# Inverse root mean squares of 128x640 blocks: logarithm and exponential on ScalarE in place of a square root there and a reciprocal on VectorE

## The reference, cut to what matters

```python
def rms_norm(x, g):
    y = xf * lax.rsqrt(jnp.mean(xf * xf, axis=-1, keepdims=True) + EPS)
    return (y * g.astype(jnp.float32)).astype(x.dtype)
...
    d = uf - jnp.mean(uf, axis=-1, keepdims=True)                       # group_layer_norm, 4 groups of 64
    y = (d * lax.rsqrt(jnp.mean(d * d, axis=-1, keepdims=True) + EPS)).reshape(bsz, t, ch)
...
    o_gla = rms_norm(o_f + jnp.flip(o_b, 1), p['gla_norm_g'][l]) * jax.nn.silu(heads(gg, GLA_DV))
    u = jax.nn.silu(group_layer_norm(u, p['conv_norm_g'][l], p['conv_norm_b'][l]))
    qa = rms_norm(heads(aq, HEAD_DIM), p['q_norm_g'][l])
    ka = rms_norm(heads(ak, HEAD_DIM), p['k_norm_g'][l])
```

## Time and profile before

| | before |
|---|---|
| median of three runs | 4559.03 us (4555.75 to 4562.23) |
| profiled execution, its own time | 4560.16 us |
| span of that execution | 4558.4 us |
| mean granted TensorE clock | 0.817 of 2.4 GHz |
| busy: PE, DVE, ACT, POOL | 2964.4, 2789.8, 954.6, 2699.0 us |
| DMA traffic | 1450.20 MB, mean 318 GB/s |

### The profile page before, as it was taken

How to read it: one execution, slowest core, us unless ns; L and a number is a source line. 1 busy time by engine, 2 the same in 40 slices (tenths; PEclk the granted TensorE clock), 3 DMA queues, 4 the chain that set the end, 5 groups by cost and what they waited for, 6 DMA issues and landing times.

```text
span 4558.4 us, 50026 instructions
## 1 busy us (share of the span) xinstructions
PE 2964.4 (65%) x17354; PEld 1289.0 (28%) x17354; DVE 2789.8 (61%) x6337; ACT 954.6 (21%) x2379; POOL 2699.0 (59%) x2760
## 2 busy tenths in 40 slices
PE   6997855566655565666578968455556665555555
PEld 4565521122211221222134655111212122212111
DVE  3515457667676677667535363676667766766673
ACT  2134012212221222122121331122122212211221
POOL 3700027777777777777748000577777777777775
PEclk9998678777788877877789968788878778888878
DMA  6532239999999999999931102799999999999998
GB/s 217 182 113 94 84 141 409 409 409 407 404 408 404 405 406 406 406 405 403 403 128 35 38 3 83 298 409 408 409 404 403 406 402 409 402 408 406 405 405 349
DMA packets 471181, 1450.20 MB, mean 318 GB/s; under 512 B 54165, under 2 KB 131345, under 8 KB 470801
## 3 DMA queue, kind: packets, MB, share of 16 engines
q0 software_dynamic: 368640, 1342.34, 74.4%
q1 hardware_dynamic: 102290, 104.66, 7.1%
HBM read 1443.62 MB, written 3.21 MB: 317 GB/s over the span
## 4 chain that ended last, share of the span: by engine, by line
PE 26%; DMA 23%; DVE 22%; POOL 15%; issue 11%; DVEq 2%; ACT 1%; SPq 0%; ACTq 0%; POOLq 0%
PE ps L551 25%; DMA arena<-in_peer_u,expert_rows 13%; DVE arena L1454 9%; DMA arena<-in_peer_v,expert_rows 9%; POOL arena L526 7%; POOL arena L534 7%; PE ps L686 1%; DVE arena L1402 1%; DVE arena L1371 1%; DVE top_indices L1401 1%; DVE arena L1433 1%; DVE arena L1436 1%; DVE chosen_pair L1438 1%; DVE top_values L1404 1%; DVE best_positions L1401 1%
## 5 line engine op out<-in xcount | busy, mean ns | idle before, releaser
L551 PE MATMUL ps<-arena 64*64 64x512 f32 (+5 forms) x14768 | 2740.3, 679 | 1430.7 <-issue 1175.7
L1454 DVE CUSTOM_DVE_ANT_0 arena<-arena,ps 128x1024 f32<-128x1024 f32 x1280 | 1526.7, 1219 | 891.3 <-DMA arena<-in_peer_u,expert_rows 887.9
L551 PEld LDWEIGHTS ps<-arena 64*64 64x64 f32 (+2 forms) x14768 | 1136.7, 179 | 3018.4 <-issue 2904.8
L526 POOL DMA_INDIRECT arena<-in_peer_u,expert_rows x1280 | 1217.9, 952 | 686.0 <-issue 306.7
L534 POOL DMA_INDIRECT arena<-in_peer_v,expert_rows x1280 | 1211.0, 946 | 412.2 <-issue 358.2
L1184 ACT ACTIVATE arena<-constants,expert_weight 128x64 f32<-128x64 f32 x1280 | 380.3, 339 | 1402.5 <-PE ps L551 1378.5
L513 POOL MEMSET arena<- 128x5632 f32 x2 | 9.6, 4792 | 372.8 <-ACTq L257 372.8
L1299 DVE TENSOR_REDUCE score_max<-ps 128x1 f32<-128x640 f32 (+1 forms) x80 | 57.4, 718 | 246.8 <-PE ps L551 246.8
L506 POOL TENSOR_SCALAR arena<-arena,vec_columns 128x512 f32<-128x512 f32 x120 | 150.4, 1264 | 10.2 <-issue 10.2
L515 POOL MEMSET arena<- 128x2048 f32 x2 | 3.6, 1806 | 226.7 <-DVEq L257 226.7
L1111 ACT ACTIVATE arena<-ps 128x256 f32<-128x256 f32 x80 | 30.7, 384 | 457.8 <-PE ps L551 444.2
(11 more groups left out here) (162 smaller groups left out, 1819.2 us busy)
## 6 DMA issues: line engine op xcount, KB each, us to landing
arena<-in_ada_w SPq DMA_DIRECT2D x40, 1024.0 KB
arena<-in_peer_u,expert_rows POOLq DMA_INDIRECT x1280
arena<-in_peer_v,expert_rows POOLq DMA_INDIRECT x1280
arena<-in_w_in SPq DMA_DIRECT2D x32, 512.0 KB, 4.1
arena<-in_ada_w SPq DMA_DIRECT2D x4, 2048.0 KB, 18.7
arena<-in_w_out SPq DMA_DIRECT2D x4, 2048.0 KB, 7.6
arena<-in_peer_wq SPq DMA_DIRECT2D x2, 4096.0 KB, 18.7
peer_modulation<-modulation_rows SPq DMA_DIRECT2D x4, 1536.0 KB, 11.5
```

The lines of the kernel that those rows point to most:

```text
L526: pool.indirect_dma_start(UR[:, k % RING, :], None, u_rows, bass.IndirectOffsetOnAxis(ap=rows[:, g % LIVE, k:k + 1], axis=0))\
L551: return pe.matmul(out, lhsT, rhs, start=start, stop=stop)
L1454: dve.tensor_tensor_reduce(out=UR[:, k % RING, :], in0=UR[:, k % RING, :], in1=pair(1), scale=1.0, scalar=0.0, op0=ALU.mult, op1=ALU.add, ...
```

## The change

The square root of mean plus epsilon becomes a logarithm, and a second activation raises e to minus a half of it, in place; that is the inverse root at once. DVE's reciprocal of the block goes. The small reciprocals (of 128x5 values, lines 1225 and 1482) and the square roots ahead of them stay.

```diff
                 def deviation(u):
                     act.wait_ge(S["var_ps"], NU * l + u + 1)
                     if u:
                         act.wait_ge(S["n_ready"], NU * l + u)
-                    act.activation(SD, pair(0)[:, 0:NTOK], ACT.Sqrt, bias=eps_c[:, 0:1]).then_inc(S["sd_ready"], 1)
+                    st.link(act.activation(SD, pair(0)[:, 0:NTOK], ACT.Ln, bias=eps_c[:, 0:1]))
+                    act.activation(SD, SD, ACT.Exp, scale=-0.5).then_inc(S["sd_ready"], 1)
...
                 for ct in range(2):
                     act.wait_ge(S["cx_var"], 2 * l + ct + 1)
-                    act.activation(CSQ[:, ct, :], zp(ct)[:, 0:NTOK], ACT.Sqrt, bias=eps_c[:, 0:1])\
-                        .then_inc(S["cx_sd"], 1)
+                    st.link(act.activation(CSQ[:, ct, :], zp(ct)[:, 0:NTOK], ACT.Ln, bias=eps_c[:, 0:1]))
+                    act.activation(CSQ[:, ct, :], CSQ[:, ct, :], ACT.Exp, scale=-0.5).then_inc(S["cx_sd"], 1)
...
                 for hp in range(2):
                     act.wait_ge(S["og_var"], 2 * l + hp + 1)
-                    act.activation(OSD[:, hp, :], pair(hp)[:, 0:NTOK], ACT.Sqrt, bias=eps_c[:, 0:1])\
-                        .then_inc(S["og_sd"], 1)
+                    st.link(act.activation(OSD[:, hp, :], pair(hp)[:, 0:NTOK], ACT.Ln, bias=eps_c[:, 0:1]))
+                    act.activation(OSD[:, hp, :], OSD[:, hp, :], ACT.Exp, scale=-0.5).then_inc(S["og_sd"], 1)
...
                     dve.wait_ge(S["sd_ready"], NU * l + u + 1)
-                    st.link(dve.reciprocal(SD, SD))
                     stt(src, src, vec[:, g:g + 1], SD, ALU.mult, ALU.mult).then_inc(S["n_ready"], 1)
...
                     dve.wait_ge(S["cx_sd"], 2 * l + ct + 1)
-                    st.link(dve.reciprocal(CSQ[:, ct, :], CSQ[:, ct, :]))
...
                     dve.wait_ge(S["og_sd"], 2 * l + hp + 1)
-                    st.link(dve.reciprocal(OSD[:, hp, :], OSD[:, hp, :]))
```

## The result

The changed kernel takes 4573.7 us (median of nine runs, 4568.63 to 4575.44), the kernel before 4559.72 (nine runs, 4555.75 to 4562.23): 14.0 us or 0.3% more, ratio 1.003 with a 95% interval of 1.002 to 1.004. The profiled execution took 4568.63 us, the shortest of the nine.

What follows compares the result with a forecast made beforehand. PE bounds the projections with ACT's root on its path, DVE bounds GLA, transfers the experts. Longer projections +25.0, GLA's first part -16.7, its end -7.6, clock +10.3 make +11.0: 4571.2 us, 4570 to compare; range 4551 to 4578.

Steps and rivals of the forecast that it cites:

- The bound and where the edits lie on it: Projections: PE bounds, with ACT's root on its path; GLA: DVE bounds; expert stages: transfers, untouched by the change.
- The reciprocals: 18 of 4.15 us each: nothing gained from the projections' ten; first part of GLA saves 8.36 us a layer, 16.7 in all.
- ACT's cover: First part of GLA: twelve exponentials start 3.1 us later yet end 4 us before DVE asks; failure costs at most 3.1 a layer.
- The tables: Logarithm and exponential evict each other, a 1.283 us load before nearly each, some 28 more; projection paths grow 25.0 us in all.
- The added load of the small root: Line 1140: about 1.3 us of load, taken as 0 because PE later waits for key copies; bounds 0 and 1.3 a layer.
- The end of GLA: Second reciprocal goes but ACT becomes late in DVE's place; 3.8 us saved a layer, 7.6 in both.
- The stalls: Projections: PE's eight waits for the inverse root become 5.04 us each, about 40 us in all.
- The clock: PE's clock falls behind the projections' eight stalls: 1.5 us each, bounds 0 and 1.7; net +10.3 us, between -1.7 and +11.9.
- the sum: Whole kernel: +25.0 - 16.7 - 7.6 + 10.3 = +11.0 us on the profiled 4560.16, giving 4571.2; time to compare 4570.
- The holding clock: Rival, chance 0.22: PE's clock stays at 2.4 GHz behind the projections' stalls; +0.7 or less, about 4559 us, no change.
- One table: Rival, chance 0.15: the build keeps one table with logarithm and exponential for projections and GLA; about 4538 us, faster.
- Dearer loads: Rival, chance 0.03: chained table loads cost twice the price for the 20 on the path; +26, about 4596 us.

Runs made afterwards that it cites:

- The filled stalls: Changed kernel with 16 unread PE products put into each of the four stalls of the second layer's projection; 4567.11 us, 1.0014 of the kernel before.
- the early release: Changed kernel, but PE's next mean of squares waits for the logarithm alone, not the exponential behind it; 4548.54 us, ratio 0.9976 to the kernel before.
- one table: Changed kernel with the table holding logarithm and exponential loaded three times a layer where ACT has time; 4533.88 us, ratio 0.9944 to the kernel before.
- one table in GLA alone: Kernel before with the change only in GLA, the table holding both functions loaded ahead of attention and behind line 1090; 4532.16 us, ratio 0.9942.

## Why the prediction was right, point by point

**The bound and where the edits lie on it.** PE in the projections and DVE in GLA, as read. The two kernels with half of the change each give +39.5 and -25.6 us.

**The reciprocals.** Nothing was to be gained from the ten in the projection, and nothing was: PE's stalls are all behind ACT. The first part of GLA was to save 8.36 us a layer; it saved 8.0 and 8.4. ACT's cover held: its twelve exponentials start 3.1 us later, as worked out (8.03 us behind the first running sum, 4.96 before), and no product of DVE waits for one.

**The tables.** 28 loads more (205 against 177), with the first logarithm of GLA finding its table loaded, as the argument from the earlier trace rows has it. The added load of the small root is hidden: PE still waits for the key copies there, 2.14 us as in the earlier trace rows. The Trainium skill, "ScalarE: Activation LUTs", section "Table sets: the hidden batching unit", says that one set holds logarithm and exponential; the trace with the set loaded by hand agrees, and in the changed kernel, where nobody asked for it, it wasn't used. The drain of about 1380 ns that the Trainium skill, "ScalarE: Activation LUTs", section "What ACT_TABLE_LOAD costs", adds to each load would have made the stalls 2 x 1.38 us longer. The trace disagrees: they are 5.04 or 5.03, without it.

**The end of GLA.** 3.8 us a layer were forecast and 3.9 measured.

**The stalls.** 5.04 us each and some 40 in all were forecast; eight of 5.04 or 5.03, 40.3 in all, were there.

**The clock is the term that was too small.** I took 1.5 us a stall from four rows and set the upper bound at 1.7. Summed over the eight stalls of the profiled execution (each product group against its time at 2.4 GHz) the loss was 16.1 us, 2.0 a stall, with single losses from 1.4 to 3.1; less the 1.75 that the kernel before paid, that is +14.3 where the sum had +10.3 and its bound +11.9. The medians of the change in the projections alone say the same: 39.5 us, less 25.0 of longer stalls, plus the 1.75, are 16.2. The filled stalls show that this is the clock.

The step that failed is the bound. Three cases that had lost 1.7 each were taken for the most that a stall can cost. The first stall alone cost 2.9 (2.48 + 3.64 against 1.25 + 1.95). That a longer stall costs more each time is not shown: with the early release a stall of 2.98 us cost 2.9 as well (4.18 + 2.84 against 2.18 + 1.96), and the seven that lost clock there lost 1.75 on average. The loss also differs between executions of the same code: the first layer's four stalls cost 8.1 us in the changed kernel and 10.5 in the one that fills only the second layer's.

With 2.0 a stall the sum is 4575.2 for the profiled execution and 4574 for the median, against 4573.7. That this fits so closely is in part luck, for the profiled execution itself took 4568.63: its projections were longer by 36.2 us and not 39, because the kernel before happened to lose clock at 215 us, where the changed one didn't, and its output projections and experts were 4.2 us shorter, for which the sum has no term.

**The rivals.** The holding clock is refuted by eight losses of eight. One table is refuted for this kernel and confirmed as a price: 4538 was worked out, and 4533.88 measured when it was made so. Its sum had the stalls 6.4 us longer in all; they were 3.3 longer (18.7 for 15.4), because the load that unit 0 had before goes too. Dearer loads are refuted: 1283 ns for each.

## What to carry to other kernels

An operation that moves from one engine to another is worth what it frees on the bounding engine of each stage: the same edit cost 39.5 us where ACT lay on PE's path and gave 25.6 where DVE did, and the best first step was to make half of it. Where two functions alternate on ScalarE, look for a load ahead of each in the trace and load the table that holds both by hand; and where a wait protects a shared PSUM bank, let the last reader release it and not the last instruction of the chain. A stall in front of PE is to be priced with the clock behind it, here 2 us on top of each 5.

## What the runs showed of the hardware that was not expected

How often PE's clock was lower behind a stall, counted over the unfilled stalls behind lines 990 and 991 in the projections of all the profiled executions here: behind 1.55 to 1.57 us in none of 34 cases (five kernels), behind 2.34 us in five of eight (one table), behind 2.98 to 3.00 us in ten of 14 (seven of eight with the early release, three of the six first stalls in three kernels that keep the roots in the projections), behind 5.04 us in all 20 (three kernels). The middle two can't be told apart by these counts. The same stall of 2.99 us, between the same products, lost clock in one execution and not in another: neither of the two in the kernel with one table in GLA alone did, both in the kernel with the change in GLA alone. Nor does the length of one stall settle it: elsewhere in the projection of the kernel before, behind stalls of 1.48 and 0.27 us at 212 to 215 us, 64 chunk products took 3.64 us and not 1.95.
